# Dense feed-forward of a two-layer hybrid block: each pair of a gate tile and an up tile as seven block products instead of eight

## What is computed

```python
def swiglu(t, w_gu, w_down):
    g, u = jnp.split(t @ w_gu, 2, axis=-1)
    return (jax.nn.silu(g) * u) @ w_down
...
        if l % 2 == 0:
            f = swiglu(h2, ffn_w_gu[l // 2], ffn_w_down[l // 2])
```

## Time and profile before

| | us |
|---|---|
| median of three runs | 1390.84 |
| lowest, highest | 1389.04, 1391.88 |
| profiled execution, its own time | 1384.94 |
| its span on the core | 1383.1 |

### The profile page before, as it was taken

One profiled execution on the slowest core, in us unless ns is written; L12 is line 12 of the kernel. 1 busy time (PEld: TensorE's weight loads), 2 busy tenths in 40 slices (PEclk: granted clock), 3 DMA queues, 4 the chain that ended last, 5 costly groups with the idle time before them and its releaser, 6 DMA issues.

```text
span 1383.1 us, 19620 instructions
## 1 busy us (share of the span) xinstructions
PE 1283.0 (93%) x7072; PEld 1012.5 (73%) x7072; DVE 812.3 (59%) x1185; ACT 685.8 (50%) x977; POOL 116.6 (8%) x86
## 2 busy tenths in 40 slices
PE   5999976899999999999999976788999999999997
PEld 1788743458688888888877964476888888888876
DVE  2322687753532332322335377666988988988896
ACT  5423352642622211322325344355877877887784
POOL 2200000003011100111120000011000000000070
PEclk9999988899999999999999997899999999999999
DMA  9432255256123321323312443627999999999995
GB/s 360 147 109 90 92 198 184 99 180 255 61 92 101 131 73 61 107 91 123 106 53 85 141 133 137 244 105 285 402 354 375 387 369 351 403 371 354 393 381 209
DMA packets 96847, 283.30 MB, mean 205 GB/s; under 512 B 8704, under 2 KB 10256, under 8 KB 96528
## 3 DMA queue, kind: packets, MB, share of 16 engines
q1 hardware_dynamic: 90880, 264.27, 53.2%
q0 software_dynamic: 3600, 12.58, 2.4%
q10 hardware_dynamic: 2304, 5.58, 1.0%
HBM read 270.86 MB, written 11.53 MB: 204 GB/s over the span
## 4 chain that ended last, share of the span: by engine, by line
PE 81%; DVE 8%; ACT 5%; DMA 3%; issue 2%; SPq 0%; ACTq 0%; DVEq 0%
PE ps L746 13%; PE ps L748 13%; PE ps L747 13%; PE ps L1177 6%; PE ps L1178 6%; PE ps L1179 6%; PE ps L1194 3%; PE ps L1196 3%; PE ps L1192 3%; PE ps L723 2%; DMA raw<-in_w_mod 2%; PE ps L840 2%; PE ps L839 2%; PE ps L841 2%; PE ps L1009 1%
## 5 line engine op out<-in xcount | busy, mean ns | idle before, releaser
L627 DVE TENSOR_TENSOR wlo<-raw,whi 128x1024 fp32r<-128x1024 f32 (+2 forms) x271 | 351.1, 1311 | 262.0 <-ACT whi L622 260.3
L622 ACT ACTIVATE whi<-raw 128x1024 fp32r<-128x1024 f32 (+2 forms) x271 | 298.2, 1107 | 217.2 <-PE ps L748 138.1
L746 PE MATMUL ps<-hhi,whi 128*128 128x512 f32 (+1 forms) x736 | 275.8, 375 | 5.5 <-DVE hlo L1822 3.7
L747 PE MATMUL ps<-hlo,whi 128*128 128x512 f32 (+1 forms) x736 | 273.0, 371 | 0.0
L748 PE MATMUL ps<-hhi,wlo 128*128 128x512 f32 (+1 forms) x736 | 273.0, 371 | 0.0
L746 PEld LDWEIGHTS ps<-hhi,whi 128*128 128x128 f32 x736 | 138.9, 189 | 39.1 <-issue 9.5
L748 PEld LDWEIGHTS ps<-hhi,wlo 128*128 128x128 f32 x736 | 138.9, 189 | 26.0
L747 PEld LDWEIGHTS ps<-hlo,whi 128*128 128x128 f32 x736 | 139.0, 189 | 25.3
L627 DVE TENSOR_TENSOR xlo<-raw,xhi 128x1024 fp32r<-128x1024 f32 (+1 forms) x98 | 134.5, 1376 | 29.0 <-ACT xhi L622 28.2
L622 ACT ACTIVATE xhi<-raw 128x1024 fp32r<-128x1024 f32 (+1 forms) x98 | 114.3, 1167 | 37.8 <-PE ps L1196 19.6
L1177 PE MATMUL ps<-whi,hs_hi 128*128 128x512 f32 (+1 forms) x256 | 95.4, 373 | 0.9 <-DVE hs_lo L2185 0.9
(11 more groups left out here) (321 smaller groups left out, 2060.0 us busy)
## 6 DMA issues: line engine op xcount, KB each, us to landing
raw<-in_w_gu SPq DMA_DIRECT2D x230, 512.0 KB, 5.9
raw<-in_w_dn SPq DMA_DIRECT2D x80, 704.0 KB, 8.3
raw<-in_w_mod SPq DMA_DIRECT2D x68, 512.0 KB, 4.5
raw<-in_w_fm SPq DMA_DIRECT2D x32, 512.0 KB, 3.5
raw<-in_w_out SPq DMA_DIRECT2D x16, 512.0 KB, 4.0
y_rows<-zrow POOLq DMA_DIRECT2D x1, 5120.0 KB, 20.7
mraw<-in_w_mod SPq DMA_DIRECT2D x8, 512.0 KB, 6.7
raw<-in_w_tg SPq DMA_DIRECT2D x8, 512.0 KB, 3.5
```

The costliest lines, as they stand in the source:

```text
L622: nc.scalar.activation(high(v)[:, 0:cols], src[:, 0:cols], ACT.Copy).then_inc(hi_ready, 1)
L627: nc.vector.tensor_tensor(low(v)[:, 0:cols], landed_in(v)[0][:, 0:cols], high(v)[:, 0:cols].bitcast(F32), ALU.subtract).then_inc(lo_ready, 1)
L746: nc.tensor.matmul(outp, whs, xh, start=first, stop=False)
L747: nc.tensor.matmul(outp, whs, xl, start=False, stop=False)
```

## The change

A pair (gate tile, up tile), two halves of k and two halves of the tokens make eight block products of 128 x 512 by 512 x 256. The new kernel makes them as seven (Winograd's form of Strassen's scheme): four sums of weight blocks per pair (`weight_sum`, on POOL, into S1 to S4, which lie in `sq` and `xn`), four sums of activation blocks once (`h_sums`, on DVE, with x12, x22 and t3 on POOL), seven products of 4 steps of k by 256 tokens (`part_product`), and five additions per pair that put the quarter results together (`combine`, on DVE). Activation block B12 of `hhi` and `hlo` is overwritten by t1. The parts of a pair are p = 7n + x, x from 0 to 6; each is a 128 x 512 piece of weights, and `whi` and `wlo` become a ring of eight such pieces. At each part (n, x) ACT and DVE make the high and low part of the piece eight ahead. The products x = 1, 3, 4 and 6 take their weights from S2, S3, S1 and S4, the others straight from `raw`.

The first two pairs of block 0 stay as they were (J0 = 2, 0), so 9 and 11 pairs have the new form (JN). The transposes of the two groups of modulation columns move from r = 6 and 8 to r = 1 and 2, ahead of the space that the new operands take. For the same reason four loads of modulation units (`norm2u`) move from ahead of the stage to the second block's down tiles. Some semaphores of the two layers are merged, with counts that go on from layer to layer (left out below).

```diff
+        def wide(x, a):
+            return fsum[:, x, a:a + 2, :].rearrange("p a (b n) -> p (a b) n", n=CTX)
+
+        x12, x22, t3 = wide(1, 9), wide(1, 7), wide(1, 5)
+        t1, t2, t4 = wide(0, 9), wide(0, 7), wide(0, 5)
+        B11, B12, B21, B22 = [(slice(4 * a, 4 * a + 4), slice(CTX * b, CTX * b + CTX)) for a in range(2) for b in range(2)]
+        whf = whi[:, :, :].rearrange("p h n -> p (h n)")
...
-        TURN_AT = {6: NORM1[1] // 2 + 1, 8: NORM1[3] // 2 + 1}
+        TURN_AT = {1: NORM1[1] // 2 + 1, 2: NORM1[3] // 2 + 1}
...
+        J0, JN, G0 = (2, 0), (FJ - 2, FJ), (0, FJ - 2)
+        PARTS = 7
+        S2, S1, S3, S4 = sq[:, 0, :], sq[:, 1, :], xn[:, 0, :], xn[:, 1, :]
+        S_OF = {1: (S2, 2), 3: (S3, 3), 4: (S1, 1), 6: (S4, 4)}
+        V0 = V_FFN[0]
...
+        def part_hi_of(act, i, p):
+            n, x = p // PARTS, p % PARTS
+            kind, q = before_part(i, p)
+            if kind == "part":
+                counted(act, part_done, split_used, i, q)
+            else:
+                act.wait_ge(split_used, i * BLOCK + V0 + q + 1)
+            if x in S_OF:
+                act.wait_ge(wsum_ready, 4 * (G0[i] + n) + S_OF[x][1])
+            else:
+                unit_landed(act, i, unit_of(i, n, x == 5))
+            q = place7(i, p)
+            count_one(nc.scalar.activation(whf[:, 512 * q:512 * q + 512], part_source(i, p), ACT.Copy),
+                      part_hi, hi_ready, p)
...
                         sp.dma_start(raw[:, slot, 0:n], src).then_inc(landed[slot], 16)
+                sp.wait_ge(split_used, (blocks - 1) * BLOCK + v0 + 2 * FJ)
+                for unit in norm2u:
+                    dst, arrived, _count = mod_landed(unit[1], unit[2])
+                    sp.dma_start(dst, source(unit)[0]).then_inc(arrived, 16)
...
+            def part_product(i, p):
+                n, x = p // PARTS, p % PARTS
+                g = G0[i] + n
+                counted(pe, part_lo, lo_ready, i, p)
+                if g == 0:
+                    if x in (0, 2):
+                        pe.wait_ge(fh_ready[0], {0: 1, 2: 2}[x])
...
+                    pe.wait_ge(first_out, g)
+                elif x in (1, 3, 4, 6):
+                    pe.wait_ge(comb_out, 5 * (g - 1) + {1: 1, 3: 2, 4: 4, 6: 5}[x])
...
+                          (lambda k: tm[:, k, :], lambda k: tm[:, 4 + k, :]),
+                          (lambda k: hhi[:, 4 + k, 0:CTX], lambda k: hlo[:, 4 + k, 0:CTX]),
+                          (lambda k: tm[:, 8 + k, :], lambda k: tm[:, 12 + k, :]),
+                          (lambda k: hhi[:, k, CTX:T], lambda k: hlo[:, k, CTX:T]),
+                          (lambda k: mr4[:, k, :], lambda k: tm[:, 16 + k, :] if k < 2 else rs2[:, k - 2, :]),
+                          (lambda k: hhi[:, 4 + k, CTX:T], lambda k: hlo[:, 4 + k, CTX:T])][x]
+                bank = (0, 2, 1, 5, 4, 3, 6)[x]
+                for k in range(4):
+                    c = 512 * place7(i, p) + P * k
+                    mm = three(ps[:, bank, 0:CTX], whf[:, c:c + P], wlf[:, c:c + P], xh(k), xl(k),
+                               k == 0, k == 3)
+                count_one(mm, part_done, split_used, p)
...
+                                mod_turns(TURN_AT[r])
+                    for p in range(PARTS * JN[i]):
+                        part_product(i, p)
+                    pe.wait_ge(comb_out, 5 * (G0[i] + JN[i] - 1) + 4)
                     for m in range(KT):
...
+                    if i == 0:
+                        t_hi(tm[:, 0:4, :], t2, t_ready, 2)
+                        t_hi(tm[:, 8:12, :], t3, hsum_ready, 3)
...
+                        if r == 0:
+                            split_hi(act, v0 + r + H, UNIT, i)
+                        if r == 3:
+                            act.wait_ge(split_used, v0 + 4)
+                            t_hi(hhi[:, B12[0], B12[1]], t1, t_ready, 1)
+                            act.wait_ge(modT_done, NORM1[3] // 2 + 1)
+                            t_hi(mr4[:, :, :], t4, t_ready, 3)
+                        for p in first_parts(r):
+                            part_hi_of(act, i, p)
+                        if r % 2 == 1:
+                            up_hi(l, i, j)
...
+                        for x in range(PARTS):
+                            if x == 0:
+                                if i * FJ + j >= 2:
+                                    act.wait_ge(flo_ready[l], i * FJ + (j - 1))
+                                counted(act, part_done, split_used, i, PARTS * n)
+                                nc.scalar.activation(hf[:, j % 2, 0:CTX], ps[:, 0, 0:CTX], ACT.Copy
+                                                     ).then_inc(first_out, 1)
+                            if PARTS * n + x + 8 < PARTS * JN[i]:
+                                part_hi_of(act, i, PARTS * n + x + 8)
+                            if x == 1 and n:
+                                up_hi(l, i, j - 1)
+                            if x == 6:
+                                gate_silu(l, i, n)
...
+            def weight_sum(i, n, m):
+                g = G0[i] + n
+                a1, a2 = (landed_in(unit_of(i, n, up))[0] for up in range(2))
+                out, in0, in1, op, x = [(S1, a2[:, 0:512], a2[:, 512:1024], ALU.add, 4),
+                                        (S2, S1, a1[:, 0:512], ALU.subtract, 1),
+                                        (S3, a1[:, 0:512], a2[:, 0:512], ALU.subtract, 3),
+                                        (S4, a1[:, 512:1024], S2, ALU.subtract, 6)][m]
+                if m < 2:
+                    unit_landed(pool, i, unit_of(i, n, 1 - m))
+                if g:
+                    counted(pool, part_lo, lo_ready, *((i, PARTS * (n - 1) + x) if n else (0, PARTS * (JN[0] - 1) + x)))
+                if m in (1, 3):
+                    pool.wait_ge(wsum_ready, 4 * g + m // 2 + 1)
+                nc.gpsimd.tensor_tensor(out, in0, in1, op).then_inc(wsum_ready, 1)
+
+            def up_lo(l, i, j):
+                pool.wait_ge(fhi_ready[l], i * FJ + (j + 1))
+                nc.gpsimd.tensor_tensor(flo[:, j, :], hf[:, j % 2, :], fhi[:, j, :].bitcast(F32),
...
+                pool.wait_ge(hlo_done, 2 * KT)
+                for out, (ks, cs) in ((x12, B12), (x22, B22)):
+                    nc.gpsimd.tensor_tensor(out, hhi[:, ks, cs].bitcast(F32), hlo[:, ks, cs].bitcast(F32), ALU.add
+                                            ).then_inc(hsum_ready, 1)
+                pool.wait_ge(hsum_ready, 2)
+                nc.gpsimd.tensor_tensor(t3, x22, x12, ALU.subtract).then_inc(hsum_ready, 1)
+                for m in range(4):
+                    weight_sum(0, 0, m)
+                for j in range(J0[0]):
+                    up_lo(l, 0, j)
                 for i in range(blocks):
-                    for j in range(FJ):
-                        pool.wait_ge(fhi_ready[l], i * FJ + (j + 1))
-                        nc.gpsimd.tensor_tensor(flo[:, j, c0:T], hf[:, j % 2, c0:T], fhi[:, j, c0:T].bitcast(F32),
-                                                ALU.subtract).then_inc(flo_ready[l], 1)
+                    for n in range(JN[i]):
+                        if n + 1 < JN[i]:
+                            for m in range(4):
+                                weight_sum(i, n + 1, m)
+                        elif i + 1 < blocks:
+                            pass
+                        if n:
...
+            def h_sums():
+                h1, l1 = hhi[:, B11[0], B11[1]].bitcast(F32), hlo[:, B11[0], B11[1]].bitcast(F32)
+                h2, l2 = hhi[:, B21[0], B21[1]].bitcast(F32), hlo[:, B21[0], B21[1]].bitcast(F32)
+                dve.wait_ge(mod_used, NORM1[-1] + 1)
+                dve.wait_ge(hsum_ready, 1)
+                then(V.tensor_tensor(t1, x12, h1, ALU.subtract))
+                V.tensor_tensor(t1, t1, l1, ALU.subtract).then_inc(t_ready, 1)
+                dve.wait_ge(hsum_ready, 2)
+                dve.wait_ge(t_ready, 1)
+                V.tensor_tensor(t2, x22, t1, ALU.subtract).then_inc(t_ready, 1)
+                dve.wait_ge(t_ready, 2)
+                then(V.tensor_tensor(t4, h2, t2, ALU.subtract))
+                V.tensor_tensor(t4, t4, l2, ALU.add).then_inc(t_ready, 1)
+                t_lo(tm[:, 4:8, :], t2, tm[:, 0:4, :], 1)
+                t_lo(tm[:, 12:16, :], t3, tm[:, 8:12, :], 2)
...
+            def combine(l, i, n, x):
+                g, j = G0[i] + n, J0[i] + n
+                p1, u3, u2 = hf[:, j % 2, 0:CTX], hf[:, j % 2, CTX:T], sg[:, j % 2, CTX:T]
+                if x >= 2:
+                    counted(dve, part_done, split_used, i, PARTS * n + x)
+                if x == 2:
+                    dve.wait_ge(first_out, g + 1)
+                    V.tensor_tensor(sg[:, j % 2, :].rearrange("p (a n) -> p a n", a=2), ps[:, 1:3, 0:CTX],
+                                    p1.rearrange("p (a n) -> p a n", a=1).broadcast_to([P, 2, CTX]), ALU.add
+                                    ).then_inc(comb_out, 1)
+                if x == 3:
```

(63 more changed lines are left out.)

259 lines of the change are left out of this document (169 added, 90 removed).

## The result

The changed kernel takes 1408.36 us (median of 4, 1406.02 to 1412.1) against 1391.36 of the kernel before beside it (median of 4, 1389.04 to 1393.01): ratio 1.0121, 95% interval 1.0104 to 1.0137, 17 us slower. The sign and the whole stated range (1378 to 1410) of the prediction hold; its size, +5 us, does not, and the forecast's own range (1394 to 1401) doesn't either.

A forecast was written before the change was run, and what follows sets the result against it. PE's pace bounds the dense stage; after the change, DVE and POOL taking turns on SBUF reads would. Start +15.3, clock +3.3, block 1 -11.3, block 0 -2.3: +5.0 on 1390.84, forecast 1395.8 us, range 1378 to 1410.

The forecast's parts named there:

- the forecast's own range: Whole kernel: a period per pair from 10.4 to 10.8 us gives +3 to +10, 1394 to 1401 us.
- The mechanism: Dense stage: DVE and POOL operations with both inputs in SBUF take turns, making a pair 10.5 us against PE's 9.52.
- The start: Block 0's start: `h_sums` ahead of unit 3's low part delays tile r = 3, +15.3 us; lost clock, +3.3.
- Rival 1: Dense stage: the port is no bound and PE sets the pace, -13.0 us, 1377.8; chance 0.22.
- Block 1: Second block's new pairs and wait at the end: 111.9 us against 123.2, -11.3.
- The ring is full at its start ... 1.4: Block 1's start: ring filled under block 0's down tiles, 69 positions left, DVE begins after the first product, 1.4 us.
- The period: One new pair in the blocks: 10.5 us, with bounds 9.52 (PE alone) and 11.3.
- there are five, one in each turn: Each new pair: all five DVE combines, 2.2 us, lie beside POOL's five operations, one per turn.
- rival 3: Dense stage: POOL falls out of step with the combines, period 11.3 us, +19.2, 1410.0; chance 0.18.
- The tail: Block's end: PE waits for DVE's remaining work before down tile 0, 7.0 us.
- Block 0: First block: 9.0 us until DVE's first position, 82.5 for 55 positions, 7.0 at the end; 98.5 against 100.8, -2.3.
- 17.72 P: Whole net change as a function of the pair's period P: 17.72 P - 181, zero at P = 10.2.

The follow-up runs named there:

- both: The changed kernel with weight sums on VectorE and unit 3's low part and `mods_in` ahead of `h_sums`; 0.7 to 0.8% faster than before, dense stage 352.09 us.

## Why the prediction was right in direction and wrong in size

**The mechanism held.** DVE and POOL take turns on operations with both inputs in SBUF, and that makes DVE the engine PE waits for. The changed kernel shows it in both places that were named, the run without reads takes the sums' part of it away, and the run with the sums on DVE does so with the work kept. By the rule of the Trainium skill (SBUF — State Buffer, section Who interferes with whom) a fill without a read, or an operation with an input in PSUM, leaves DVE alone; the 692 ns beside MEMSET and the combines' 0.68 agree.

**The start was right, its two parts within about 1 us.** Predicted: tile r = 3 starts 24.0 us after N (386.0 - 361.96), 15.3 late, and the clock costs 3.3 more, 18.6 in all. Measured: PE waits 15.3 us for the modulation group, needs 0.7 for the transposes and starts r = 3 at 393.17, 24.9 after N, so 16.1 late; the tile then takes 7.5 us instead of 5.6. That is 1.9 for the clock, and the second `hf` is 18.1 later from N than before. Of the 0.8 that the wait is longer, DVE's addition for `mod` explains the most: it takes 1.02 us (391.27) beside POOL's `flo` where it takes 0.17 alone (401.67).

**Rival 1 named a floor that PE doesn't reach.** PE's pace was put at 9.52 us a pair, from 24 matmuls of another stage. It is 9.92. The forecast didn't use it, as it went by DVE, but even without the port the change has only 25.6 us to give in place of 33.6.

**The terms that were mis-sized are those of the two blocks.** Block 1 was put at 111.9 (-11.3) and takes 120.3, between the two `xT` without the 7.7 of a down tile. Three terms:

- "The ring is full at its start ... 1.4". It isn't: DVE makes the last parts only behind the last down tile, and by then POOL's sums of the next pair begin. Behind the last down tile of block 0 in the changed kernel, DVE and then POOL:

```profile
563.99 0.88 DVE L2430 SCALAR_TENSOR_TENSOR xT<-ps,mod,xT 128x256 f32<-128x256 f32 x2 [5.63 <-PE ps L864]
564.78 0.68 DVE L603 TENSOR_TENSOR wlo<-sq,whi 128x512 fp32r<-128x512 f32 x1
565.38 0.68 DVE L603 TENSOR_TENSOR wlo<-raw,whi 128x512 fp32r<-128x512 f32 x1
565.99 1.78 DVE L603 TENSOR_TENSOR wlo<-xn,whi 128x512 fp32r<-128x512 f32 x1
567.69 1.78 DVE L603 TENSOR_TENSOR wlo<-raw,whi 128x512 fp32r<-128x512 f32 x1
...
565.61 1.61 POOL L1884 TENSOR_TENSOR sq<-raw 128x512 f32<-128x512 f32 x1 [34.62 <-DVE wlo L603]
```

  Four parts were still to be made. DVE is through with them at 569.5, 5.5 us behind the down tile: +4.1. In `both` the same four parts stand behind the down tile too, but meet no sum of POOL's and take 2.4 us (545.39 to 547.80) instead of 4.7. No run moves these parts ahead of the tile.
- The period. The 69 positions take 106.1 us, 10.76 a pair instead of 10.5: +2.6. (In the middle a pair takes 10.93; the last one, for which POOL has no sums left, is shorter.) The step that was wrong is "there are five, one in each turn": I had let all five combines, 2.2 us, lie beside POOL. Three do (x = 2, 5 and 6, 1.54 us). Five turns hold DVE back by 1.1 each (1.70 against its pace of 0.60), 5.5; less 1.5 that is 4.0, and 3.9 is measured. The combines of x = 3 and 4, 0.33 each, add to the 10.3 of bare turns: 10.97, measured 10.93. That is rival 3 in part: its bound of 11.3 has two combines outside POOL's turns too, those of x = 2 and 3.
- The tail takes 8.8 instead of 7.0: +1.8. The 7.0 to the start of the first down tile was right (675.41, DVE's last low part done, to 682.44). But I had taken the down tile itself as before. From its first matmul to its `xT` it takes 9.55 us (682.44 to 691.99) where it took 7.90 (662.21 to 670.11), 1.65 more. PE has just waited 2.4 us, behind a block with many short waits, and the granted clock goes down to 0.50:

```profile
684.00:686.00 2.00, 2.00 (x6) 1.60 (x5) 0.25 (x1) 1.71 (x2) 0.00 (x0) 0.50 0.60 142
```

Block 0 was put at -2.3 and comes out at +0.3 with the same three terms, smaller: DVE's first position 9.9 instead of 9.0, 10.61 a pair, tail 8.3. There the clock stays at 1.00 in the first down tile, although PE has waited 2.3 us ahead of it, and 0.8 of its extra 1.2 us is a wait for POOL's last `flo`. (By the positions it is 101.6 us, by the marks of the table 101.1.) Together the two blocks miss by 11.0 us; with the start 0.5 under its sum that is the whole difference between +5.0 and the dense stage's +15.5. With the net depending on the period as 17.72 P, the sum was near a zero crossing, where small terms decide; the own range of +3 to +10 let only P vary and held the fill and the tail fixed. Those two make 8.1 of the 11.6 that the terms add up to.

**Luck in the range.** The measured +17 lies inside the stated range only because rival 3, with +19, was in it. Rival 3 had all of that from a period of 11.3. Measured is 10.76 and 10.61, which makes 3.5 us of the miss (2.6 and 0.9); the other 8.1 came from the fill and the tail, which no rival varied.

**The share of the page misleads here.** PE is busy 67.03 of 70 us in block 0, and one might look for 4% at most. But the row has 553 matmuls, and at 0.118 us they are 65.3 us of work, so 7% is lost; in block 1 it is 66.43 shown for 64.4 of work. In the records each of these matmuls lasts 0.28 us, while the next one can start after 0.118, so about the first 0.16 us of every wait is shown as busy.

## What to carry to other kernels

Before an algorithm with fewer products is fed by sums on GpSimd, look at which of the new operations and of VectorE's old ones read both inputs from SBUF: add one turn of both for each meeting, and compare with PE's pace. The sums may cost less on the engine that is already busy all the time: here 2.4 us of work a pair put onto VectorE took 3.4 us of blocking off it (3.9 before; one `wlo<-xn` longer by 0.5 is left), and with the start put in order a change that lost 1.2% became one that wins 0.7%. When a buffer of finished parts is meant to be full at a stage's start, check who fills it and behind what; and when the start of a stage is a backlog of one engine, reordering helps only until that engine has no gap. Behind a wait of PE, look at the granted clock of what follows before taking its length as unchanged.
